# Transposing an expert's gathered tokens: eight prompt transposes and then eight sample transposes, in place of alternating ones

## The reference

```python
def expert_choice(xn, w_router, w_eg, w_eu, w_ed):
    C = CAPACITY_FACTOR * T // N_EXPERTS            # prompt: 128, sample: 64
    aff = softmax(xt @ w_router, axis=-1)
    gate, idx = lax.top_k(aff.T, C)                 # each expert picks C tokens
    xe = xt[idx]
    h = silu(einsum('ecd,edf->ecf', xe, w_eg)) * einsum('ecd,edf->ecf', xe, w_eu)
    ye = einsum('ecf,efd->ecd', h, w_ed) * gate[..., None]
    out = zeros((T, D)).at[idx.reshape(-1)].add(ye.reshape(-1, D))
```

## Time and profile before

| what | value |
|---|---|
| median of 3 runs | 3467.32 us (3466.83 to 3471.26) |
| the profiled execution (its span, the one time there is of it) | 3481.5 us |
| TensorE busy | 3295.9 us, 95% |
| TensorE weight loads | 2868.7 us, 82% |
| VectorE busy | 1858.5 us, 53% |
| ScalarE busy | 1433.8 us, 41% |
| mean DMA rate | 156 GB/s over the span |
| mean granted TensorE clock | 0.952 of full |

### The profile page before, as it was taken

The page is one execution under the profiler, slowest core; times in us unless marked ns, Lnnn a source line. Parts: engine busy times, 40 slices in busy tenths (PEclk is TensorE's granted clock), DMA queues, the critical chain, the costliest instruction groups (busy, mean ns, idle before and its releaser), DMA issues. The chain is left out here.

```text
span 3481.5 us, 45734 instructions
## 1 busy us (share of the span) xinstructions
PE 3295.9 (95%) x17656; PEld 2868.7 (82%) x17656; DVE 1858.5 (53%) x2770; ACT 1433.8 (41%) x1969; POOL 122.3 (4%) x133
## 2 busy tenths in 40 slices
PE   6999999999999999985999999999999999999994
PEld 4978989896487786544999999999999999999993
DVE  4140221305334332276677777777776777777774
ACT  4030120312333321323555555655565555555553
POOL 0000000000000000000000000000000000000000
PEclk9969979699999999986999999999999999999997
DMA  4000000003132335223677767777677767776774
GB/s 161 25 32 25 14 18 25 31 13 109 44 98 87 95 121 175 91 79 130 227 235 239 241 220 245 235 239 231 238 244 234 241 229 237 234 242 222 246 227 160
DMA packets 456895, 543.03 MB, mean 156 GB/s; under 512 B 13131, under 2 KB 372811, under 8 KB 456684
## 3 DMA queue, kind: packets, MB, share of 16 engines
q1 hardware_dynamic: 449644, 516.71, 44.1%
q0 software_dynamic: 7168, 25.17, 3.2%
HBM read 502.37 MB, written 39.47 MB: 156 GB/s over the span
## 5 line engine op out<-in xcount | busy, mean ns | idle before, releaser
L1432 PE MATMUL ps<-xsplit,wh 128*128 128x384 f32 x4096 | 1168.9, 360 | 2.2 <-DVE xsplit L1527 2.2
L1434 PE MATMUL ps<-xsplit,wl 128*128 128x192 f32 x4096 | 1026.6, 251 | 0.0
L1520 DVE TENSOR_TENSOR wl<-raw,wh 128x2048 fp32r<-128x2048 f32 x384 | 876.7, 2283 | 116.4 <-ACT wh L1477 115.3
L1477 ACT ACTIVATE wh<-raw 128x2048 fp32r<-128x2048 f32 x384 | 734.1, 1912 | 349.1 <-PE ps L1456 323.2
L1434 PEld LDWEIGHTS ps<-xsplit,wl 128*128 128x128 f32 x4096 | 784.0, 191 | 0.6
L1432 PEld LDWEIGHTS ps<-xsplit,wh 128*128 128x128 f32 x4096 | 770.2, 188 | 3.0 <-issue 2.4
L1491 ACT ACTIVATE low<-ps 128x384 f32<-128x384 f32 x256 | 126.0, 492 | 435.4 <-PE ps L1434 435.4
L1536 DVE TENSOR_TENSOR gu<-ps,low 128x384 f32<-128x384 f32 x256 | 142.8, 558 | 221.1 <-ACT low L1491 220.0
L1049 DVE TENSOR_TENSOR glow<-graw,ghigh 128x1024 fp32r<-128x1024 f32 x72 | 88.1, 1225 | 235.7 <-ACT ghigh L1005 235.7
L549 PE MATMUL ps<-whigh,xhigh 128*128 128x256 f32 x624 | 203.7, 326 | 3.5 <-ACT u L683 2.8
L550 PE MATMUL ps<-wlow,xhigh 128*128 128x256 f32 x624 | 203.6, 326 | 0.0
(11 more groups left out here) (205 smaller groups left out, 4626.7 us busy)
## 6 DMA issues: line engine op xcount, KB each, us to landing
raw<-in_w_exp_gate_dram SPq DMA_DIRECT2D x128, 1024.0 KB, 5.6
raw<-in_w_exp_up_dram SPq DMA_DIRECT2D x128, 1024.0 KB, 7.8
raw<-in_w_exp_down_dram SPq DMA_DIRECT2D x128, 1024.0 KB, 6.9
graw<-in_w_gate_dram SPq DMA_DIRECT2D x96, 256.0 KB, 2.9
wraw<-in_w_in_dram SPq DMA_DIRECT2D x12, 1024.0 KB, 5.0
graw<-in_w_four_br_dram SPq DMA_DIRECT2D x24, 384.0 KB, 3.5
xin<-in_x_dram SPq DMA_DIRECT2D x12, 512.0 KB, 3.9
xres<-in_x_dram SPq DMA_DIRECT2D x12, 512.0 KB, 3.6
```

The lines of the kernel that those rows point to most:

```text
L1432: pe.matmul(ps[:, bank, 0:2 * CAP], wh[:, q % AHEAD, tile], xsplit[:, k, :, :].rearrange("p s t -> p (s t)"), start=k == 0, stop=False)
L1434: mm = pe.matmul(ps[:, bank, CAP:2 * CAP], wl[:, q % AHEAD, tile], xsplit[:, k, 0, :], start=False, stop=k == KT - 1)
L1477: act.activation(cut_part(wh, q), raw_part(q), ACT.Copy).then_inc(w_high, 1)
L1520: dve.tensor_tensor(cut_part(wl, q), raw_part(q), cut_part(wh, q).bitcast(F32), ALU.subtract).then_inc(w_cut, 1)
```

## The change

The body of `turn_tokens` is written with the two groups of requests in the outer loop and the eight pieces in the inner one. Operands, banks and columns of each transpose stay as they are, and so do the waits ahead. The semaphore `x_T` is raised by the sample's fourth and eighth transposes, as before; these are now the twelfth and the sixteenth of the turn, where they were the eighth and the sixteenth. The lines behind move down by one (L1432 becomes L1433, and so on).

```diff
                     pe.wait_ge(x_in, (n + 1) * 32)
                     pe.wait_ge(gu_sum, n * FT + GU_PAIRS)
-                    for k in range(KT):
-                        at_col = (k % 2) * CAP
-                        pe.transpose(ps[:, k // 2, at_col:at_col + CAPS[0]], xg[0][:, k * P:(k + 1) * P], ident[:, :])
-                        mm = pe.transpose(ps[:, k // 2, at_col + CAPS[0]:at_col + CAP], xg[1][:, k * P:(k + 1) * P],
-                                          ident[0:CAPS[1], 0:CAPS[1]])
-                        if k % 4 == 3:
-                            mm.then_inc(x_T, 1)
+
+                    for s, first in ((0, 0), (1, CAPS[0])):
+                        for k in range(KT):
+                            at_col = (k % 2) * CAP + first
+                            mm = pe.transpose(ps[:, k // 2, at_col:at_col + CAPS[s]], xg[s][:, k * P:(k + 1) * P],
+                                              ident[0:CAPS[s], 0:CAPS[s]])
+                            if s == 1 and k % 4 == 3:
+                                mm.then_inc(x_T, 1)
```

## The result

| | median | lowest to highest | runs |
|---|---|---|---|
| before | 3467.32 us | 3466.07 to 3475.64 | 5 |
| changed | 3430.57 us | 3428.06 to 3435.21 | 5 |

The ratio is 0.9888 with a 95% interval of 0.9869 to 0.9907: the change takes 36.8 us off by the medians, where 30.6 were forecast, and by the interval 32 to 45 us.

What follows compares the result with a forecast made beforehand. TensorE, busy throughout each 112.90 us loop period, was taken as the bound. Turns 24.3, first turn 1.6 and clock falls 4.7 sum to 30.6 us off the 3467.32 median: 3436.7 us, range 3429 to 3452.

Steps and rivals of the forecast that it cites:

- TensorE paces the loop: Expert loop: TensorE busy for all 112.90 us of a period, so shortening its work shortens the period as much.
- The change of row count is what costs: Inside a turn: alternating 64 and 128 rows, not the transposes, costs time; fourteen of fifteen changes are removed.
- The price of the sample's transposes: Sample's eight transposes in a turn: 1.05 us, with bounds of 0.87 and 1.60.
- The turns' term: Fifteen loop turns: 3.63 to 2.01 us each, 1.62 saved per turn, 24.3 us; bounds 16.0 and 28.4.
- The low end of the range: Whole kernel, all transposes at 0.109: 28.4 + 2.4 + 4.7 = 35.5 saved, 3431.8, less 3 for spread: 3429 us.
- The first rival, no gain on the sample: Turns: sample transposes keep 0.20 us each, so 16.0 us from the turns; time 3445.5 us; chance 0.14.
- The falls: After three of fifteen loop turns the granted clock drops to 1.2 GHz; all three vanish, saving 4.7 us.
- the fourth rival: Matmuls behind each turn: clock falls every turn and stays down twice as long; 3484.7 us, slower; chance 0.05.
- The first turn: Turn ahead of the loop, at half the clock: 5.6 to 4.0 us, 1.6 us earlier; bounds 0.8 and 2.4.
- What is late next: Behind a shorter turn: ScalarE's 3.90 us and VectorE's 2.59 us waits exceed 1.6, so nothing is lost.

Runs made afterwards that it cites:

- blocks of four: Changed kernel with each turn as four prompt, four sample, four and four transposes, three changes of row count instead of one: 3435.01 us, 0.9908 to before.
- twelve transposes: Against the changed kernel, the sample's 64 tokens gathered as 128 half-width rows, so four 128x128 transposes replace its eight: 3430.80 us, 0.9893 to before.

## Why the prediction was right, and where it was wrong

**TensorE paces the loop, and a turn stands on its path whole: right.** The period fell by what the turn fell, and repeating a turn gives its length back (110.89, 112.55, 114.21).

**The change of row count is what costs: right, and shown.** Take it away and alternating costs nothing (1.66 us a turn); put one pair back and 0.29 us come back. I read the mixed matmuls of the earlier trace rows as changing at every step; they change at every second, and a pair of changes costs some 0.3 there too.

**The price of the sample's transposes: wrong, and this step made the forecast too small and let the range end too soon on the fast side.** I took six inner steps of 0.109 and a first and last of 0.20, 1.05 us, and even gave 0.109 as the lower bound, "since their weights have 128 columns too". The sample took 0.63. Its inner steps are 0.062, its first is 0.11 and its last 0.15. So the bound did not bind: neither the 128 columns of weights nor the uniform matmuls of the earlier trace rows tell the step of a 64-row transpose. The turns' term was 24.3 and measured 15 x 2.01 = 30.2, more than the 28.4 that I took as the most it could be. The low end of the range, 3429, was added up from that 28.4; with 30.2 the same sum gives 3427. The 5.9 us come close to the 6.2 by which the medians (36.8) exceed the forecast (30.6). With an interval of 32 to 45 us that closeness is luck; the size of the step is shown by the trace.

The Trainium skill, "TensorE: Matmul & The Clock Gate", Part 2, LDWEIGHTS, gives a load's time by its columns alone, whatever its rows; by its formula an estimate for 128 columns is 107 ns. Eight 64-row loads of 128 columns in 0.57 us disagree. The Trainium skill, "TensorE: Matmul & The Clock Gate", Part 2, Back-to-back issue gap, has for moving operands of up to 64 columns a floor of about 25 ns per matmul, and about 62 ns with hardware decode off. The sample's steps of 62 ns agree with the second number, but no run here shows which decoding was at work, or that a floor is what sets the step.

**The first rival, no gain on the sample: refuted.** Loads that use rows 0 to 63 again and again go ahead too (eight in 0.57 us).

**The falls: the effect right in the trace, the reason wrong, so that this term, as far as it came true, did so by luck.** Three falls went, 4.7 us by the profiles; the times can't confirm them. I argued that a turn of 2.01 us is shorter than 2.58 us of the routing stage without one. The turns of 4.92 us without a fall show that shortness wasn't needed. For the same reason the fourth rival, falls at every turn, had the matter upside down: behind long stretches of grouped transposes the clock stayed up in every trace. The Trainium skill, "TensorE: Matmul & The Clock Gate", Part 4, has it that transposes don't count as busy in the same way; that a stretch of 4.92 us of nothing else left the clock at 1.00 in all fifteen turns does not bear it out.

**The first turn: about right, as far as single traces tell.** 1.6 forecast; 1.3 by the kernel that changes only this, 2.8 between the two profiles, with the clock's rise in it.

**Sum from the first turn on:** 30.2 for the turns, 4.7 for the falls, 2.8 for the first turn: 37.7 of the 38.0 us between the profiles.

**What is late next: right, nothing.** The slack shrank by 1.1 to 1.2 us and was enough. With 1.7 us (blocks of four) to 2.4 us (twelve transposes) taken from every period, no wait took TensorE's place.

## What to carry to other kernels

On TensorE, look for neighbouring instructions whose weights have different row counts: compare the distance of starts there with that of a uniform row elsewhere in the same trace, and see whether the weight load starts before or with its own matmul. Group the two kinds, or pad the smaller to the larger; both gave the same here, at 0.29 us for each pair of changes. When no row shows the shape that the change puts together, a bound taken from another shape isn't a bound, so leave the range open on that side.

## What the runs showed of the hardware beyond that

- Transposes of 64 rows next to each other start 0.062 us apart at full clock, those of 128 rows 0.109. At half the clock (the first turn with the change) it is 0.107 and 0.213: there the smaller take half the time of the larger, at full clock more than half. Eight of 64 rows, with the change to 128 rows behind, took 0.63 us; the same tokens packed into four of 128 rows took 0.36.
- Transposes in rows of eight, for 4.92 us with a pause only at each change of row count, did not let the granted clock fall in any of fifteen turns; alternating ones, for 3.63 us with a pause at every step, did in three of fifteen. Each is one trace.
- A change of row count cost about the same for transposes and for attention's matmuls: 0.29 and some 0.3 us a pair.
- Stages that a change does not touch differed by 15 us between two profiled executions (the first turn at 1611.12 and at 1595.97; from 100 to 700 us the granted clock was 0.86 in the one and 0.88 in the other). Two traces are best compared from the point where the kernels begin to differ.
